# Hybrid encoder step on one core: the recurrent branch's weight products are moved into the attention steps, and w_out is split beside the attention branch's products

## The reference, cut to what matters

```
h = rmsnorm(x) @ w_in                  # 45 column tiles of 128 are needed
oa = differential attention, 4 heads: softmax(q1 k1) - lambda * softmax(q2 k2), times v
oa = rmsnorm(oa) * 0.8 * silu(da_gate)                        # (T, 512)
ob = gated linear attention (recurrence), 4 heads; rmsnorm(ob) * silu(gla_gate)   # (T, 512)
g_a, g_b = split(sigmoid(merge_logits))                       # (T, 1024) each
mixed = g_a * (oa @ w_branch_a) + g_b * (ob @ w_branch_b)     # w_branch_*: 512 x 1024
y = rmsnorm(x + mixed @ w_out)                                # w_out: 1024 x 1024
```

## Time and profile before

| what | value |
| --- | --- |
| median of three runs | 997.5 us |
| profiled execution, its own time | 997.8 us |
| its span, first to last instruction | 995.9 us |
| mean granted TensorE clock | 0.987 |
| PE busy | 951.8 us (96%) |
| DVE busy | 483.6 us (49%) |
| ACT busy | 327.3 us (33%) |

### The profile page before, as it was taken

How to read it: one execution, slowest core, us unless ns; L and a number is a source line. 1 busy time by engine, 2 the same in 40 slices (tenths; PEclk the granted TensorE clock), 3 DMA queues, 4 the chain that set the end, 5 groups by cost and what they waited for, 6 DMA issues and landing times.

```text
span 995.9 us, 15321 instructions
## 1 busy us (share of the span) xinstructions
PE 951.8 (96%) x6204; PEld 878.3 (88%) x6204; DVE 483.6 (49%) x1107; ACT 327.3 (33%) x775; POOL 42.3 (4%) x77
## 2 busy tenths in 40 slices
PE   5999999999999999999999999999999799979997
PEld 4999999999999999989889898989999599978884
DVE  6532366661216566425635463555556755561222
ACT  6453322222233322224443443444344412130110
POOL 1000000000000000000000000000000000000000
PEclk9999999999999999999999999999999799989999
DMA  8012011213110102341204011210222564431221
GB/s 306 16 46 64 22 44 43 88 43 94 43 43 23 54 27 65 90 147 39 65 2 118 14 52 49 70 44 22 70 61 87 169 191 161 148 122 48 85 102 56
DMA packets 86167, 75.51 MB, mean 76 GB/s; under 512 B 3681, under 2 KB 77810, under 8 KB 85970
## 3 DMA queue, kind: packets, MB, share of 16 engines
q1 hardware_dynamic: 86098, 74.54, 24.2%
HBM read 54.81 MB, written 19.73 MB: 75 GB/s over the span
## 4 chain that ended last, share of the span: by engine, by line
PE 90%; DVE 4%; ACT 2%; issue 2%; DMA 1%; POOL 0%; SPq 0%; POOLq 0%; ACTq 0%; DVEq 0%
PE proj_bank L1296 18%; PE proj_bank L1298 17%; PE proj_bank L1297 17%; PE score_banks L1296 6%; PE score_banks L1297 6%; PE score_banks L1298 6%; PE turn_bank L1511 4%; PE score_banks L1478 4%; PE score_banks L1415 2%; PE turn_bank L1495 2%; PE score_banks L1391 1%; PE turn_bank L1429 1%; PE turn_bank L1377 1%; PE turn_bank L1432 1%; PE score_banks L1392 1%
## 5 line engine op out<-in xcount | busy, mean ns | idle before, releaser
L1296 PE MATMUL proj_bank<-x_hi,w_hi 128*128 128x352 f32 x1080 | 358.1, 332 | 0.5 <-DVE w_lo L561 0.5
L1298 PE MATMUL proj_bank<-x_hi,w_lo 128*128 128x352 f32 x1080 | 349.1, 323 | 0.0
L1297 PE MATMUL proj_bank<-x_lo,w_hi 128*128 128x352 f32 x1080 | 348.5, 323 | 0.0
L1296 PEld LDWEIGHTS proj_bank<-x_hi,w_hi 128*128 128x128 f32 x1080 | 205.0, 190 | 2.7 <-issue 1.8
L1297 PEld LDWEIGHTS proj_bank<-x_lo,w_hi 128*128 128x128 f32 x1080 | 205.1, 190 | 0.0
L1298 PEld LDWEIGHTS proj_bank<-x_hi,w_lo 128*128 128x128 f32 x1080 | 204.5, 189 | 0.0
L561 DVE TENSOR_TENSOR w_lo<-w_raw,w_hi 128x1024 fp32r<-128x1024 f32 x53 | 64.8, 1223 | 85.0 <-ACT w_hi L557 84.9
L911 ACT ACTIVATE probs<-score_banks,softmax_stats 128x128 f32<-128x128 f32 (+8 forms) x72 | 51.2, 712 | 77.8 <-DVE softmax_stats L1188 72.9
L1296 PE MATMUL score_banks<-branches_hi,w_hi 128*128 128x352 f32 x192 | 64.5, 336 | 2.4 <-DVE branches_lo L1169 2.3
L1296 PE MATMUL score_banks<-w_out_hi,mixed_hi 128*128 128x512 f32 (+2 forms) x160 | 60.3, 377 | 5.6 <-DVE w_out_lo L561 5.6
L819 ACT ACTIVATE feature_stage<-proj_bank 128x352 f32<-128x352 f32 x48 | 22.3, 464 | 127.8 <-PE proj_bank L1298 127.8
(11 more groups left out here) (159 smaller groups left out, 1218.2 us busy)
## 6 DMA issues: line engine op xcount, KB each, us to landing
w_raw<-in_w_in SPq DMA_DIRECT2D x45, 512.0 KB, 4.4
merge_tanh_scratch<-feature_stage SPq DMA_DIRECT2D x16, 528.0 KB, 3.1
feature_stage<-merge_tanh_scratch SPq DMA_DIRECT2D x8, 528.0 KB, 4.2
merge_tanh<-merge_tanh_scratch SPq DMA_DIRECT2D x8, 528.0 KB, 4.1
x_rows<-in_x_prompt SPq DMA_DIRECT2D x8, 512.0 KB, 7.7
branch_out<-in_x_prompt SPq DMA_DIRECT2D x8, 512.0 KB, 3.6
out<-branch_out SPq DMA_DIRECT2D x8, 512.0 KB, 2.6
gla_branch_scratch<-branch_out SPq DMA_DIRECT2D x1, 2112.0 KB, 8.1
```

What stands on the lines that cost most here:

```text
L1296: nc.tensor.matmul(out, wh, xh, start=first, stop=False)
L1297: nc.tensor.matmul(out, wh, xl, start=False, stop=False)
L1298: return nc.tensor.matmul(out, wl, xh, start=False, stop=last)
```

## The change

The merge is taken apart into 24 `bunit`s and 24 `aunit`s of 12 matmuls each.

- `bunit` (recurrent branch, `proj_bank`s): PE multiplies, DVE multiplies by the gate in one instruction and leaves the result in a new tile `mix_b` (`MB`). 14 of the 24 lie in attention steps, counted by `shares` at half a projection unit; the projection units move to earlier steps. `DRAIN` puts 2, 3 and 3 in the three drain steps and 2 behind them. The recurrent output comes back in one DMA (`obload`) and is split by thirds right behind the last projection tile's units.
- `aunit` (attention branch, all four `score_banks`): PE multiplies; DVE multiplies by the gate, adds `mix_b`, and writes the lo part of the unit before; ACT writes hi.
- Weight tiles of a branch now hold two feature tiles. `LATE` is the order in which the late tiles are split: four of the recurrent branch, four of the attention branch, eight of w_out. `A_SPLITS` says before which `aunit` the last eleven are split, all eight of w_out among them; w_out's halves have space of their own. All late tiles go through the two raw buffers.
- The merge gates come one tile at a time into the two `feature_stage` buffers (`gate` stages), the first when the last `mg` tile has been stored.
- The output products wait only for the mixed tiles that they read.

The resulting order at the end, worked out from the new `stage_list`: the last projection unit (44.2) lies in step (3, 4), with `mgout`, `gate 0`, `bsplit 2`, `gate 1`, `split` and `bunit 0.0` behind it, then `aO.3.1`, `aC.3.4`, `aQ.3.2`. Step (3, 5) has four `bunit`s, (3, 6) three, (3, 7) three with `asplit 0` behind them, (3, 8) three with `asplit 1`.

```diff
@@ -30,13 +30,15 @@
-NBS = 2 * H - 1 + 3
...
-TAIL = (3, 3, 4)
+DRAIN = (2, 3, 3, 2)
+A_SPLITS = {0: 0, 1: 1, 3: 2, 6: 3, 8: 4, 10: 5, 11: 6, 13: 7, 15: 8, 17: 9, 19: 10}
+LATE = [("b", 0), ("b", 1), ("b", 2), ("b", 3), ("a", 0), ("a", 1), ("o", 0), ("o", 1), ("a", 2), ("o", 2), ("o", 3), ("o", 4),
+        ("a", 3), ("o", 5), ("o", 6), ("o", 7)]
 STEPS = H * NTT
...

     def unit(kind, i, th):
+        if kind == "b":
+            if th == 0:
+                stages.append(("gate", i + 1))
+                if i % 2 == 0:
+                    stages.append(("split", len(tiles) + i // 2 + 1))
+            stages.append(("bunit", i, th))
...
+                    stages.append(("gate", 0))
+        if t == len(tiles) - 1:
+            stages.append(("bsplit", th))

     part = {name: [(k, i, th) for k, i in v for th in range(3)] for name, v in phases().items()}
...
+    b_units = [("b", f, th) for f in range(KD_) for th in range(3)]
+    last = len(b_units) - sum(DRAIN)
+    cost = [(u, 2) for u in part["att"]] + [(u, 1) for u in b_units[:last]]
+    halves = [u for u, c in cost for _ in range(c)]
+    fill, seen = [], set()
+    for part_ in shares(halves, [100 - load(s) for s in range(STEPS)]):
+        fill.append([u for u in dict.fromkeys(part_) if u not in seen])
+        seen.update(part_)
     for s in range(STEPS):
         h, i = divmod(s, NTT)
-        if s == STEPS - 2:
-            stages.append(("bload", 0))
-            stages.append(("bload", 1))
+        if s == NTT:
+            stages.append(("obload",))
         if i == 4 and h + 1 < H:
             stages.append(("vload", h + 1))
-        step(s, fill[s])
+        more = [("asplit", s - STEPS + 2)] if s >= STEPS - 2 else []
+        step(s, fill[s], more)
+        assert not (s == STEPS - 3 and part["att"][-1] not in seen)
     flush()
-
-    stages.append(("bload", 2))
-    stages.append(("split", len(tiles) + 1))
-    pieces = [("bsplit", n) for n in range(NBS - 1)]
-    pieces[1:1] = [("bload", 3)]
-    for i, n in enumerate(TAIL):
-        if i == 2:
-            stages.append(("merge", 0))
-        step(STEPS + i, [], pieces[:n])
-        del pieces[:n]
-    stages.append(("bsplit", NBS - 1))
+    for n in range(3):
+        units = b_units[last:last + DRAIN[n]]
+        last += DRAIN[n]
+        step(STEPS + n, units, [("asplit", 2), ("asplit", 3)] if n == 0 else [("asplit", 4)] if n == 1 else [])
+    stages.append(("asplit", 5))
+    for u in b_units[last:]:
+        unit(*u)
+    for v in range(3 * KD_):
+        if v % 3 == 0 and v < 3 * KD_ - 3:
+            stages.append(("gate", KD_ + 1 + v // 3))
+        if v in A_SPLITS:
+            stages.append(("split", len(tiles) + 5 + A_SPLITS[v]))
+        stages.append(("aunit",) + divmod(v, 3))
...
+            if kind == "in" and w >= 2 or kind == "b" and i < 2:
                 act_.wait_ge(s_unit, units_done(w - 2))
-            nc.scalar.activation(halves(w)[0], raw_slot(w), ACT.Copy).then_inc(s_whi, 1)
+            elif kind == "b":
+                act_.wait_ge(s_bunit, 6 * (i - 1))
+            elif kind == "a" and i < 2:
+                act_.wait_ge(s_bunit, 6 * (i + 3))
+            elif kind == "a":
+                act_.wait_ge(s_aunit, 6 * (i - 1))
+            elif kind == "o" and i == 0:
+                freed(act_, ("aO", H - 1, NTT - 1))
+                act_.wait_ge(s_tmst, 32 * 2 * H)
+            elif kind == "o" and i == 4:
+                act_.wait_ge(s_bunit, 3 * KD_)
+            nc.scalar.activation(halves(w)[0], raw[w % 2][:, :, :], ACT.Copy).then_inc(s_whi, 1)
...
+                elif kind == "obload":
+                    sp.wait_ge(s_obst, 16)
+                    sp.dma_start(t_["OBS"][:, :, :].rearrange("p h t -> p (h t)"), ob_dram).then_inc(s_obld, 16)
+                elif kind == "gate":
+                    n = st[1]
+                    if n < 2:
+                        for s in range(NFT):
+                            sp.wait_ge(s_mgst[s], 16 * seen[s])
+                    elif n <= KD_ + 1:
+                        sp.wait_ge(s_bout, 3 * (n - 1))
                     else:
-                        sp.wait_ge(s_bl, 1)
-                    sp.dma_start(OBX[k], ob_dram[:, T * k:T * (k + 1)]).then_inc(s_obld[k], 16)
+                        sp.wait_ge(s_mixa, 3 * (n - KD_ - 1))
+                    sp.dma_start(FT[n % 2][:, :], tanh_dram[KD_ * (1 - n // KD_) + n % KD_, :, :]).then_inc(s_tld[n % 2], 16)
...
+            sp.wait_ge(s_aunit, 3 * KD_)
+            for i in range(2):
+                sp.dma_start(OAB_rows[i][0:ntok(i), :], x_rows(i)).then_inc(s_xres[i], 16)
...
+                    cols = slice(TH * st[1], TH * (st[1] + 1))
+                    act.wait_ge(s_unit, unit_no(NP_ - 1, st[1]) + 1)
+                    act.wait_ge(s_obld, 16)
+                    nc.scalar.activation(BHB[:, :, cols], t_["OBS"][:, :, cols], ACT.Copy).then_inc(s_bh, 1)
+                elif kind == "asplit":
+                    h, t0, t1, upto = pieces[st[1]]
+                    act.wait_ge(s_bl, 3)
+                    freed(act, ("aO", h, upto - 1))
+                    nc.scalar.activation(BHA[:, h, t0:t1], OAB[:, h, t0:t1], ACT.Copy).then_inc(s_ah, 1)
+                elif kind == "aunit":
+                    f, th = st[1], st[2]
+                    v = 3 * f + th
+                    act.wait_ge(s_mix, v + 1)
+                    nc.scalar.activation(MXH[:, f, TH * th:TH * (th + 1)], mixw[v % 2][:, :], ACT.Copy).then_inc(s_mxh, 1)
...
+                elif kind == "bunit":
+                    f, th = st[1], st[2]
+                    u = 3 * f + th
+                    cols = slice(TH * th, TH * (th + 1))
+                    dve.wait_ge(s_bunit, u + 1)
+                    dve.wait_ge(s_tld[f % 2], 16 * (f // 2 + 1))
+                    nc.vector.scalar_tensor_tensor(out=MB[:, f, cols], in0=FT[f % 2][:, cols], scalar=1.0, in1=PJ[u % 2][:, 0:TH],
+                                                   op0=ALU.add, op1=ALU.mult).then_inc(s_bout, 1)
+                elif kind == "aunit":
+                    f, th = st[1], st[2]
+                    v = 3 * f + th
+                    cols = slice(TH * th, TH * (th + 1))
+                    dve.wait_ge(s_aunit, v + 1)
+                    if v == 0:
+                        dve.wait_ge(s_tmst, 32 * 2 * H)
+                    if v >= 2:
+                        dve.wait_ge(s_mxl, v - 1)
+                    dve.wait_ge(s_tld[f % 2], 16 * (KD_ // 2 + f // 2 + 1))
+                    nc.vector.scalar_tensor_tensor(out=mixw[v % 2][:, :], in0=FT[f % 2][:, cols], scalar=1.0,
+                                                   in1=SC[:, v % 4, 0:TH], op0=ALU.add, op1=ALU.mult).then_inc(s_mixa, 1)
+                    dve.wait_ge(s_mixa, v + 1)
+                    dve.wait_ge(s_bout, u_last)
+                    nc.vector.tensor_tensor(mixw[v % 2][:, :], mixw[v % 2][:, :], MB[:, f, cols], ALU.add).then_inc(s_mix, 1)
+                    if v:
+                        mixed_lo(v - 1)
...
+                elif kind == "bunit":
+                    f, th = st[1], st[2]
+                    u = 3 * f + th
+                    cols = slice(TH * th, TH * (th + 1))
+                    w = NP_ + f // 2
+                    pe.wait_ge(s_wlo, w + 1)
+                    if u < 2:
+                        pe.wait_ge(s_uout, 3 * NP_)
+                    else:
+                        pe.wait_ge(s_bout, u - 1)
+                    pe.wait_ge(s_bl, min(u, 2) + 1)
+                    for k in range(H):
+                        last = three(PJ[u % 2][:, 0:TH], halves(w)[0][:, H * (f % 2) + k, :], halves(w)[1][:, H * (f % 2) + k, :],
+                                     BHB[:, k, cols], BLB[:, k, cols], k == 0, k == H - 1)
+                    last.then_inc(s_bunit, 1)
+                elif kind == "aunit":
+                    f, th = st[1], st[2]
+                    v = 3 * f + th
+                    cols = slice(TH * th, TH * (th + 1))
+                    w = NP_ + LATE.index(("a", f // 2))
+                    pe.wait_ge(s_wlo, w + 1)
+                    if v < 4:
+                        pe.wait_ge(s_ex, 2 * H * NTT)
+                    else:
+                        pe.wait_ge(s_mixa, v - 3)
+                    for k in range(H):
+                        if v < 3:
+
+                            pe.wait_ge(s_al, k + 1 + (th if k == H - 1 else 0))
+                        last = three(SC[:, v % 4, 0:TH], halves(w)[0][:, H * (f % 2) + k, :], halves(w)[1][:, H * (f % 2) + k, :],
+                                     BHA[:, k, cols], BLA[:, k, cols], k == 0, k == H - 1)
+                    last.then_inc(s_aunit, 1)
...
+                pe.wait_ge(s_mxl, 3 * KD_ - 2 + min((P * i + n - 1) // TH, 2))
...
+                    else:
+                        pe.wait_ge(s_mixa, 3 * KD_ - 3 + y)
+                    if i == 0:
+                        pe.wait_ge(s_wlo, NP_ + LATE.index(("o", 4 * e + 3)) + 1)
```

(54 more changed lines are left out.)

205 lines of the change are left out of this document (51 added, 154 removed).

## The result

| | before | changed |
|---|---|---|
| median of the comparison, us | 997.38 (996.53 to 999.14, 4 runs) | 1008.58 (1005.36 to 1009.37, 4 runs) |
| profiled execution: span (own time), us | 995.9 (997.8) | 1003.6 (1005.4) |
| its mean granted clock | 0.987 | 0.994 |
| last B product taken by VectorE, us | | 832.88 |
| first output product, us | 887.27 | 895.20 |

The ratio is 1.0103, with a 95% interval of 1.0085 to 1.0121. The change made the kernel slower: 11.2 us where I forecast 3.9. The sign was right, the size was not, and the time is above the range. The changed kernel's profiled execution is the fastest of its four runs. Its 7.9 us in the start of the output products are therefore less than the 11.2 of the medians, so I also read a second trace of the same kernel (experiment `e0_changed_again`), whose time is at its median.

The account below looks back on a forecast made before the run. PE, busy in 96% of the span, was taken as the bound. Removing 18.0 us of idle time and making 15.7+6.2 = 21.9 gave +3.9 on the median of 997.5: 1001.4 us, 8-in-10 range 992 to 1008.

Parts of the forecast that it names:

- The drain filled: In the three drain steps, B products cover PE's waits: idle time there costed at 0, bounds 0 and 6.2 us.
- The drain isn't filled: Rival: splits and gates queue before the drain's chain, so half of the 12.4 us loss stays, 1007.6 us; chance 0.05.
- The first gate: Behind the last projection unit, PE idles 5.65 us because gate 0's store and load delay DVE's combine; bounds 4.5 to 8.3.
- My second sign: Trace should show one 4.5 to 8 us hole on PE's probability transposes within 10 us of the last projection matmul.
- The predicted 1.2 GHz stretch: After the first gate's hole, PE runs 3.4 us at low clock: +1.6 us, bounds 0 and 3.2.
- The first gate costs little: Rival: the 5.65 us hole behind the last projection unit and its 1.6 don't appear, 994.1 us; chance 0.18.
- B products in attention steps: Their DVE work in attention steps is hidden by DVE's idle half; only `aX.3.7.0` comes 1.5 us late, 0 to 3.
- Regained waits: Thicker projection units in early attention steps remove PE's waits for probabilities: -2.6 us, bounds 0 and -7.
- The second phase: Attention branch's products with ten splits: 61.5 us against 45.8 for PE alone; 3.74 per split stage, 1.54 without.
- The banks absorb the splits: Rival: ACT's and DVE's lag in the attention branch's products never reaches PE, 13.5 us less, 987.9 us; chance 0.12.
- VectorE doesn't overlap: Rival: each VectorE instruction in the second phase waits for the end of the one before, 1004.0 us; chance 0.03.
- stays low in the second phase: Rival: PE's clock stays low in the attention branch's products, eight slow products giving 1006 us; chance 0.14.

Follow-up runs that it names:

- e0_changed_again: The changed kernel run again unaltered, for a second trace: 1008.11 us, 1.0113 of the kernel before.
- e2: The changed kernel with gate 0 loaded earlier, at the start of the last projection tile: 1004.16 us, 1.006 of the kernel before.
- e3: The changed kernel with the splits of the recurrent branch's output put later, off the combines: 1003.29 us, 1.0062 of the kernel before.
- e1: The changed kernel with the last ten weight splits moved one attention product earlier in ScalarE's queue alone: 1002.33 us, 1.0047 of the kernel before.
- e5: e4_all_three with four of the eleven last splits put behind the attention products and the first output products reordered: 985.62 us, 0.9883 of the kernel before.
- e6: The changed kernel with all eight w_out splits put behind the attention products: 1013.04 us, 1.0157 of the kernel before.
- e4_all_three: The changed kernel with the edits of e1, e2 and e3 together: 993.08 us, 0.9949 of the kernel before.

## Why the prediction was wrong in size, by its steps

The moment that I followed, the start of the output products, was forecast at 891.2 and came at 895.2 and 896.9. From there to the end are 108.6 us before, 108.4 in the first trace and 109.4 in e0, with its longer stretch at 1.2 GHz. "Everything behind it has the same instructions" is not quite so: the first row tile is done in 48 matmuls instead of 96, 0.4 us less.

1. *The drain filled*: right. Behind the gate's hole PE waits there only 0.89 us for probabilities, where I had put 1.5 for `aX.3.7.0`, and 0.73 for their evacuated transposes, where I had put nothing. "The drain isn't filled" falls. I had called all of the 12.4 us lost there idle time. The trace of the kernel before has 7.4 us of waits there; of the rest 4.1 are work at 1.2 GHz, 9.0 us in two stretches (781.4 to 784.8 and 788.2 to 795.1). Filling the drain took these away too: no trace of a changed kernel has such a stretch between 778 us and the end of the attention branch's products.
2. *The first gate*: right in mechanism, a size too large. 0.60 of idle time at the evacuation and 3.75 (3.60 in e0), instead of 5.65. My second sign asked for one hole of 4.5 to 8 us and failed: it is shorter, and there are two. The predicted 1.2 GHz stretch came, 1.6. "The first gate costs little" falls by e2: it cost 4.0.
3. *"B products in attention steps"* is the step that failed. I wrote: "Their DVE work is one instruction of 0.5 us per 1.9 us of PE, hidden by DVE's idle half." I counted the products' instructions and not the split of the branch's output, 1.37 us on ACT and 1.62 on DVE for a third, which the same edit puts between a projection unit and the combine. It made a hole of 2.5 us, and in e0 a stretch at 1.2 GHz: 2.5+1.6 = 4.1 forecast as 0. e3, which moves these splits only, shows it: the hole is gone and the median is 4.8 us lower, the 2.5 of idle time for certain and the rest with the clock.
4. *Regained waits*, -2.6: those for probabilities shrank from 2.6 to 0.36 in the steps ahead of the holes, but the waits for evacuated tokens and values, 2.8+1.1 before, rose to 5.2. That is -2.24+1.3 = -0.9.
5. *The second phase*, 61.5 us: measured 62.3 and 62.5. The chain was right: 3.73 to 3.74 with a split, 3.5 for the last lo part, and nine waits on PE, of 0.4 to 1.6 us where I had said 1.3 to 1.8. e1, e5 and e6, which change that chain in three ways, move the phase as it says. "The banks absorb the splits" falls. "VectorE doesn't overlap" falls too: the lo part still starts 0.45 behind the addition, as in the earlier trace rows. Of what the phase took over the forecast, about 1 us, the plain stages are 0.7: twelve at 1.60 for 1.54.
6. *The clock*: "stays low in the second phase" falls. From 850 to 880 PE is busy 22.6 of 30 us at a granted clock of 1.00. But I carried one new stretch at 1.2 GHz where the slower trace has two.

e0 starts its output products 5.7 us later than forecast. The misses of the steps, in us: step 3 +2.49 and +1.6; gate hole (0.60+3.60 for 5.65) -1.45; drain (0.89+0.73 for 1.5) +0.1; step 4 +0.36 and +1.3; step 5 +1.0; and -1.6 for the stretch of the earlier trace rows, which stood in my starting point and is in neither trace of the changed kernel. They sum to 3.8. The other 1.9 us are no waits but PE's own work. I added up, from each matmul's start to the next one's, the time that is neither a wait nor the price of 1.2 GHz (11/24 of the work done at it). From the first attention step's scores to the last projection matmul that is 332.7 us in the kernel before; from the same scores to the last B product it is 385.0 in e0 and 384.7 in the first trace. The difference, 52.3 and 52.1, stands against my 4.8+45.8 = 50.6: +1.7 in e0. B products behind one another start 1.91 us apart, as I had them from the merges, but one that follows attention work takes 1.99 to 2.02 (in e0 the next ones start at 783.21, 785.21 and 787.12). At full clock they average 1.97 us in e0, which is 24x0.06 = 1.4 of the 1.7. Why the first one takes longer no run here shows. The last 0.3 us stand ahead of all this: the scores start at 432.06 instead of 431.80.

## What to carry to other kernels

When work is moved into a stretch in which the engines are half idle, write down for each in-order queue every instruction that comes with it, its splits and casts too, and what stands behind each: it is the position that costs, not the busy share. A pair of instructions on two engines (hi part on one, lo part on the other) cost their sum here in the queue of the second, until the first engine's half was issued one stage ahead, and then only where its tile had landed. Work that blocks at one end of a phase and floods the other is best cut in two: all of w_out behind cost 12 us in one wait. All of it inside made the phase 62 us where PE alone needs 47, and still 56 with ScalarE's half of each split issued ahead; with half of it inside, also issued ahead, the phase was 49 and the wait 0.8.

## What the runs showed of the hardware that I had not expected

The same kernel doesn't fall to 1.2 GHz at the same places in every execution. The kernel before did so at 614.2 us, behind a PE busy 1.91 of 3.2 us; in its repeat PE was busy 2.12 of 3.4 us in the stretch that ends with the same wait, and no fall followed. Five traces have the changed kernel's hole of 2.5 us: behind it the first ran on at 1.00, the other four (e0, e1, e2, e6) fell. Five have the hole of 3.6 to 3.75, and all of them fell, for 3.4 us in three and 6.8 in two (e1 and e3). Beside e0, runs of the kernel before spanned 992.9, 995.8 and 998.5 us at mean clocks of 0.991, 0.987 and 0.983: most of the spread of one kernel's times goes with these stretches. A hole should therefore be priced as itself plus a chance of 1.6 us. The two kernels that closed the holes also gained that: their runs have mean clocks of 0.993 to 0.995 (`e4_all_three`) and 0.996 to 0.997 (`e5_w_out_half_later`), e0's 0.989 to 0.991.
